# Two blocks of mLSTM, Fourier, mixer and attention layers: the order of the first loads, where rms scaling is applied, and how modulation rows are gathered

## The reference, cut to what matters

```python
sh, sc, g = jnp.split(silu(c) @ w_ada[0] + b_ada[0], 3, axis=-1)        # c: (1, 1024), w_ada[0]: (1024, 3072)
h = rmsnorm(x, norm_g[0]) * (1.0 + sc[:, None, :]) + sh[:, None, :]
shc, scc, gc = jnp.split(silu(c_ctx) @ w_ada[0] + b_ada[0], 3, axis=-1)
hc = rmsnorm(ctx, norm_g[0]) * (1.0 + scc) + shc
# rmsnorm(x, g) = x * rsqrt(mean(x*x) + 1e-6) * g, the mean over the 1024 channels
xm, o_pre, z = jnp.split(hmod @ w_in, 3, axis=-1)                        # for h and for hc; w_in: (1024, 6144)
xconv = silu(conv3x3_depthwise(xm) + conv_b)                             # then q, k, gates, a chunked mLSTM scan, ...
```

## Time and profile before

| | |
|---|---|
| median of 3 runs | 1452.86 us |
| profiled execution: own time, span | 1452.27 us, 1450.5 us |
| TensorE matmul (PE) busy | 1310.4 us, 90% |
| VectorE (DVE) busy | 825.2 us, 57% |
| ScalarE (ACT) busy | 577.5 us, 40% |
| GpSimd (POOL) busy | 241.7 us, 17% |
| mean granted TensorE clock | 0.945 |
| chain that ended last | PE 80%, DVE 8%, issue 4%, ACT 2% |
| read from memory | 193.37 MB, 134 GB/s over the span |

### The profile page before, as it was taken

One profiled execution on the slowest core, in us unless ns is written; L12 is line 12 of the kernel. 1 busy time (PEld: TensorE's weight loads), 2 busy tenths in 40 slices (PEclk: granted clock), 3 DMA queues, 4 the chain that ended last, 5 costly groups with the idle time before them and its releaser, 6 DMA issues.

```text
span 1450.5 us, 23605 instructions
## 1 busy us (share of the span) xinstructions
PE 1310.4 (90%) x9584; PEld 1194.1 (82%) x9584; DVE 825.2 (57%) x1212; ACT 577.5 (40%) x872; POOL 241.7 (17%) x169
## 2 busy tenths in 40 slices
PE   2699999999996689899998989999988779899997
PEld 1489877778983479899998989999987648899996
DVE  0567663335454757654446675554469985655544
ACT  1433443324542223445235435444354244544433
POOL 0342400034460001000200121110025500011100
PEclk8799999999996889999999999999999759999999
DMA  9356321112550003454133444455523402355551
GB/s 386 136 189 239 153 87 59 58 58 77 185 183 20 1 29 122 173 182 174 59 123 139 175 145 147 175 190 187 177 99 132 145 0 88 117 176 189 186 176 57
DMA packets 28225, 195.59 MB, mean 135 GB/s; under 512 B 3176, under 2 KB 4200, under 8 KB 4848
## 3 DMA queue, kind: packets, MB, share of 16 engines
q1 hardware_dynamic: 26208, 189.80, 35.9%
q10 hardware_dynamic: 1936, 4.62, 0.9%
HBM read 193.37 MB, written 1.05 MB: 134 GB/s over the span
## 4 chain that ended last, share of the span: by engine, by line
PE 80%; DVE 8%; issue 4%; ACT 2%; DVEq 1%; POOL 0%; ACTq 0%
PE ps L381 23%; PE ps L383 23%; PE ps L382 23%; PE ps L423 3%; PE ps L587 3%; DVE acc L1771 2%; PE ps L521 1%; PE ps L524 1%; PE ps L438 1%; DVE V L1510 1%; DVE rstd L1580 1%; PE ps L575 1%; DVE wexp L1513 1%; PE ps L449 1%; ACT w_hi L804 0%
## 5 line engine op out<-in xcount | busy, mean ns | idle before, releaser
L804 ACT ACTIVATE w_hi<-ring 128x1024 fp32r<-128x1024 f32 x312 | 327.6, 1058 | 504.9 <-PE ps L383 414.7
L1287 DVE TENSOR_TENSOR w_lo<-ring,w_hi 128x1024 fp32r<-128x1024 f32 x272 | 338.6, 1253 | 321.0 <-ACT w_hi L804 320.5
L381 PE MATMUL ps<-x_hi,w_hi 128*128 128x256 f32 x1216 | 350.0, 288 | 24.8 <-DVE x_lo L1589 20.2
L382 PE MATMUL ps<-x_lo,w_hi 128*128 128x256 f32 x1216 | 348.6, 287 | 0.0
L383 PE MATMUL ps<-x_hi,w_lo 128*128 128x256 f32 x1216 | 348.5, 287 | 0.0
L381 PEld LDWEIGHTS ps<-x_hi,w_hi 128*128 128x128 f32 x1216 | 238.3, 196 | 27.5 <-issue 24.9
L382 PEld LDWEIGHTS ps<-x_lo,w_hi 128*128 128x128 f32 x1216 | 238.5, 196 | 0.0
L383 PEld LDWEIGHTS ps<-x_hi,w_lo 128*128 128x128 f32 x1216 | 238.0, 196 | 0.0
L381 PE MATMUL ps<-g_hi,w_hi 128*128 128x256 f32 x608 | 171.8, 283 | 1.8 <-POOL g_lo L1246 1.0
L383 PE MATMUL ps<-g_hi,w_lo 128*128 128x256 f32 x608 | 171.2, 282 | 0.0
L382 PE MATMUL ps<-g_lo,w_hi 128*128 128x256 f32 x608 | 170.5, 280 | 0.0
(11 more groups left out here) (296 smaller groups left out, 2170.1 us busy)
## 6 DMA issues: line engine op xcount, KB each, us to landing
ring<-in_weights SPq DMA_DIRECT2D x156, 1024.0 KB, 4.8
o_sb<-in_weights SPq DMA_DIRECT2D x10, 1024.0 KB, 6.7
z_sb<-in_weights SPq DMA_DIRECT2D x10, 1024.0 KB, 7.9
V<-in_weights SPq DMA_DIRECT2D x3, 1024.0 KB, 19.9
dft<-in_dft ACTq DMA_DIRECT2D x1, 1026.0 KB, 5.8
X<-in_x ACTq DMA_DIRECT2D x1, 1024.0 KB, 9.8
xconv<-in_ctx ACTq DMA_DIRECT2D x1, 1024.0 KB, 35.0
xconv<-in_weights SPq DMA_DIRECT2D x1, 1024.0 KB, 28.5
```

Of the source, the lines that this page charges most:

```text
L381: mm(dst, w_h, x_h, start=start, stop=False, skip_group_check=True)
L382: mm(dst, w_h, x_l, start=False, stop=False, skip_group_check=True)
L804: do(w_hi[:, q % 2, part], ring[:, q % RING, part], ACT.Copy).then_inc(S("hi_ready"), 1)
L1287: v.tensor_tensor(w_lo[:, q % 2, part], ring[:, q % RING, part], w_hi[:, q % 2, part], ALU.subtract).then_inc(S("lo_ready"), 1)
```

## The change

- SP's queue starts with x, then the context, then the modulation blocks; the two first ring slots come behind blocks 4 and 7. ScalarE's queue has c, the vectors up to the gate weights, and the constants; the gate weights and `rows` are issued behind the h tiles.
- The context lands in `ctx_room`, which is the second half of w_lo. GpSimd therefore waits, ahead of its second slot, for the scaling by rstd and for eight h tiles.
- The rows of all early blocks are gathered in one bank (5), those of all late ones in another (6): silc is a 62-column tile with its two filled columns at 30, and block `at` uses the 32 columns from 30 - 2 at, so that its two rows come out at 2 at in each row group, and all blocks add up. There is one copy and one turn for all early blocks and one for all late ones; `fold` has 32 columns.
- The sum of squares stands behind block 2. ScalarE rounds the first ring slot ahead of the modulation's copy.
- VectorE multiplies X and context by rstd in four operations of 128 x 1024 ahead of modulation; then ScalarE makes the hi part with scale and bias in one operation, and VectorE makes the same by tensor_scalar into xconv and subtracts.

```diff
+        ctx_room = tensors(ctx_stack)("ctx_room", (P, 2, KD, CTX))[:, 1]       # shares w_lo's place
@@ SP
+            sp.dma_start(X[:, :, :], x_in).then_inc(S("x_ready"), 16)
+            sp.dma_start(ctx_room, ctx_in).then_inc(S("ctx_ready"), 16)
             for a in range(N_ADA0):
                 load_ada(a)
-                if a in (5, 7):
-                    load((a - 5) // 2)
+                if a in (4, 7):
+                    load((a - 4) // 3)
@@ TensorE
-                if a >= 2:
-                    pe.wait_ge(S("ada_moved"), a - 1)
+                late = a >= N_ADA0
+                at, count = (a - N_ADA0, N_ADA1) if late else (a, N_ADA0)
                 for j in range(2):
                     for g in range(4):
-                        last = mm(ps[32 * g:32 * g + 32, 5 + a % 2, 0:SEQ], silc[:, 4 * j + g, :],
-                                  w[:, 4 * j + g, :], start=(j == 0), stop=(j == 1), skip_group_check=True)
+                        last = mm(ps[32 * g:32 * g + 32, 5 + late, 0:SEQ],
+                                  silc[:, 4 * j + g, 30 - 2 * at:62 - 2 * at], w[:, 4 * j + g, :],
+                                  start=(at == 0 and j == 0), stop=(at == count - 1 and j == 1),
+                                  skip_group_check=True)
...
+                n = 2 * (N_ADA1 if late else N_ADA0)
                 for b in range(2):
-                    col = 2 * (2 * a + b)
-                    last = mm(ps[:, 4, col:col + 2], arow[:, a % 2, b * P:(b + 1) * P], fold[:, :],
+                    col = (4 * N_ADA0 if late else 0) + n * b
+                    last = mm(ps[:, 4, col:col + n], arow[:, b * P:(b + 1) * P], fold[:, 0:n],
                               start=True, stop=True)
...
             for a in range(N_ADA0):
                 ada_rows(a)
-                if a:
-                    ada_turn(a - 1)
-                if a == 5:
+                if a == 2:
                     pe.wait_ge(S("ones_ready"), 3)
                     column_sum(ps[:, 7, :], ones_d[:, :], lambda k: V[:, k, :], KD, S("squares_0"),
                                S("meansq_0"))
-            ada_turn(N_ADA0 - 1)
+            ada_turn(0)
...
                     ada_rows(a)
-                    if a > N_ADA0:
-                        ada_turn(a - 1)
-            ada_turn(N_ADA0 + N_ADA1 - 1)
+            ada_turn(1)
@@ ScalarE
             act.dma_start(vec[:, 0:2 * KD], vec_in[:, 0:2 * KD]).then_inc(S("c_ready"), 16)
-            act.dma_start(X[:, :, :], x_in).then_inc(S("x_ready"), 16)
+            act.dma_start(vec[:, 2 * KD:gate_at], vec_in[:, 2 * KD:gate_at]).then_inc(S("vec_ready"), 16)
             act.dma_start(cst[:, :], cst_in).then_inc(S("ident_ready"), 16)
-            act.dma_start(xconv[:, 0:KD, 0:CTX], ctx_in).then_inc(S("ctx_ready"), 16)
-            act.dma_start(vec[:, 2 * KD:VECS], vec_in[:, 2 * KD:VECS]).then_inc(S("vec_ready"), 16)
-            act.dma_start(rows[:, :], row_in).then_inc(S("rows_ready"), 16)
...
+            hi(STARTS["xm"])
+            move_rows(0)
+            act.wait_ge(S("mod0_ready"), 1)
             for k in range(KD):
-                if k in (0, 3):
-                    hi(STARTS["xm"] + k // 3)
+                if k == 4:
+                    hi(STARTS["xm"] + 1)
                 for t, col, dst in ((0, 1, hc), (1, 0, hl)):
-                    act.wait_ge(S("scaled_0"), 2 * k + t + 1)
+                    act.wait_ge(S("rooted_0"), 2 * t + k // 4 + 1)
                     do(dst[:, 0, k, :], V[:, k, t * CTX:t * CTX + SEQ], ACT.Identity,
-                       bias=modl[:, k, col:col + 1]).then_inc(S("h_rounded"), 1)
+                       bias=modl[:, k, col:col + 1], scale=scl[:, t * KD + k:t * KD + k + 1])\
+                        .then_inc(S("h_rounded"), 1)
+            act.dma_start(vec[:, gate_at:VECS], vec_in[:, gate_at:VECS]).then_inc(S("gate_w_ready"), 16)
+            act.dma_start(rows[:, :], row_in).then_inc(S("rows_ready"), 16)
@@ GpSimd
-            for q in range(STARTS["xm"], STARTS["qk"] + 2):
+            lo(STARTS["xm"])
+            pool.wait_ge(S("rooted_0"), 4)
+            pool.wait_ge(S("h_ready"), KD)
+            for q in range(STARTS["xm"] + 1, STARTS["qk"] + 2):
                 lo(q)
@@ VectorE
             chain.step(v.reciprocal(rstd[:, :], rstd[:, :]))
+            chain.join()
...
+            for t, src in enumerate((ctx_room, X)):
+                for h in range(2):
+                    k = slice(KD // 2 * h, KD // 2 * (h + 1))
+                    v.tensor_tensor(V[:, k, t * CTX:t * CTX + SEQ], src[:, k, :],
+                                    wide(rstd[:, t * CTX:t * CTX + SEQ], KD // 2), ALU.mult)\
+                        .then_inc(S("rooted_0"), 1)
...
-            dve.wait_ge(S("ada_turned"), N_ADA0)
+            dve.wait_ge(S("ada_turned"), 1)
...
+            sources = [(k, *a) for k in range(KD) for a in ((0, 1, hc), (1, 0, hl))]
+            for n in range(2 * KD + 1):
+                if n < 2 * KD:
+                    k, t, col, dst = sources[n]
+                    cols = slice(t * CTX, t * CTX + SEQ)
+                    chain.step(v.tensor_scalar(xconv[:, k, cols], V[:, k, cols],
+                                               scl[:, t * KD + k:t * KD + k + 1], modl[:, k, col:col + 1],
+                                               ALU.mult, ALU.add))
+                if n:
+                    chain.join(1 if n < 2 * KD else 0)
+                    k, t, col, dst = sources[n - 1]
+                    dve.wait_ge(S("h_rounded"), n)
+                    v.tensor_tensor(dst[:, 1, k, :], xconv[:, k, t * CTX:t * CTX + SEQ], dst[:, 0, k, :],
+                                    ALU.subtract).then_inc(S("h_ready"), 1)
```

More of the change, by code:

```diff
@@ L191, in program @@
         xconv = sa("xconv", (P, KE, TOK))
-        silc, ones_row = one_place("ones_row", (HEADS, CTX), ("silc", (P, KD, 32), F32))
-        gate_parts, arow = one_place("arow", (P, 2, SEQ), ("gate_parts", (P, 2, 2 * HC, 32), F32R))
+        arow, ones_row = one_place("ones_row", (HEADS, CTX), ("arow", (P, SEQ), F32))
+        silc, gate_parts, _ = one_place("gate_room", (P, 2, 2 * HC, 32), ("silc", (P, KD, 62), F32),
+                                     ("gate_parts", (P, 2, 2 * HC, 32), F32R))
         gcol = sa("gcol", (P, 2, 4, HEADS))
-        fold = sa("fold", (P, 2))
+        fold = sa("fold", (P, 32))
         wexp = [wexp2[:, b] for b in range(2)]
@@ L887, in silu @@
                     do(a, a, ACT.Silu).then_inc(S("xconv_ready"), 1)
-            def move_rows_of(t):
-                for a in range(2):
-                    move_rows(N_ADA0 + 2 * t + a)
             for t in range(N_XM - 2):
@@ L895, in _ @@
                 move_xm(t // 2, t % 2)
-                move_rows_of(t)
                 if t >= 2:
@@ L912, in _ @@
                 move_xm(N_XM // 2 - 1, u)
-                move_rows_of(N_XM - 2 + u)
                 if u == 0:
                     round_head(0)
+                else:
+                    move_rows(1)
                 silu(N_XM // 2 - 2, u)
@@ L924, in round_gate_weights @@
             def round_gate_weights(hd):
+                if hd == 0:
+                    act.wait_ge(S("gate_w_ready"), 16)
                 if hd >= 2:
```

72 lines of the change are left out of this document (28 added, 44 removed).

## The result

The changed kernel takes **1431.07 us** (median of four runs, 1429.36 to 1432.05) against 1452.55 (four runs, 1451.67 to 1453.43): ratio 0.9852, interval 0.9841 to 0.9864, 21.5 us less. The forecast was 1424, with a range of 1419.5 to 1430, so the time lies 1.1 us outside it. The profiled execution has a span of 1429.3 us against 1450.5, so 21.2 of the forecast 28.7 us came.

The account below looks back on a forecast made before the run. TensorE's list bounds the kernel, with a chain of waits from the late context tile before the first projection. 20.25 + 0.65 + 0.93 + 6.5 + 0.4 = 28.7 us off 1452.27 gives 1423.5, as a median 1424; range 1419.5 to 1430.

Parts of the forecast that it names:

- Loads, sum, modulation: Ahead of the first projection: context lands at 8.5 to 9, block 7 at 33.7, sum takes 8.7, modulation ready at 39.2.
- Start: TensorE's first projection matmul: at 41.05 instead of 61.30, 20.25 us gained.
- Slot 0: First xm slot, 96 matmuls: 13.55 us instead of 14.2 with the same cold start, 0.65 gained; bounds 11.8 and 15.4.
- GpSimd's next pair: GpSimd's two subtractions for the second slot: in practice behind the whole h loop, done at 54.7, covered by 4 us.
- Rival (b): Sum at 1.2 GHz (+4.9), reciprocal excluded (+2.4), or GpSimd inside h loop (up to +1.9): 1426 to 1431 us; chance 0.14.
- the bound 15.4: Upper bound in us for the first xm slot, with GpSimd taking its turns inside the h loop.
- Slots 0 to 7 and their blocks: Modulation blocks behind the xm slots: fewer turns gain 0.93, 6.5 and 0.4 us; the period falls to 13.6.
- Behind qk: Everything after qk's start: the same list, moving as a block, with no further gain or loss.

Follow-up runs that it names:

- the operands of before: Against the changed kernel with scalar_tensor_tensor and no stall: both VectorE h-loop operations read two whole tensors and a scalar per partition; 1425.86 us.
- the run without a gap: Against the changed kernel: ScalarE's second w_hi is rounded behind all sixteen h tiles instead of ahead of the ninth; 1430.94 us, ratio 0.985.

## Why the prediction was wrong, step by step

- *Loads, sum, modulation.* Right. Context landed by 8.77 (8.5 to 9), block 7 by 33.48 (33.7), the sum took 7.80 (8.7, bounds 6.9 and 13.6). The reciprocal ran its 3.35 us with a GpSimd subtraction beside it, the second subtraction cost the products 2.1, and VectorE was through at 38.08 (38.8). By the Trainium skill's rule ("SBUF — State Buffer", "Who interferes with whom") a VectorE operation with a single SBUF input doesn't contend with GpSimd outside the 2-port modes, which the page says tensor_scalar can enter. For the reciprocal the trace agrees. The prediction left out the page's exception, and it matters: tensor_scalar, with one SBUF tensor, took 2.46 us at 47.02 beside GpSimd. Start: 20.87 gained against 20.25.
- *Slot 0: the term that failed.* "With the same cold start I get 13.55: 0.65 gained", bounds 11.8 to 15.4; it took 20.25, 6.05 lost. The step under it: "GpSimd's next pair stands behind eight h tiles and in practice behind the whole loop". I took that practice from GpSimd's request of before, where VectorE's operations read two tensors and a scalar; the change puts others in their place, and these let it in. Rival (b) had the mechanism, at 0.14, but with "up to +1.9", one turn, as has the bound 15.4, and on the condition of a gap, which the run without a gap refutes. It was three turns of about 2 us each, and then the second cold start. Holding GpSimd back brought slot 0 to 13.7 us and gave 8.1 us in all, and the operands of before alone 2.5 us of slot 0 from one kernel to the other with a milder case (two turns).
- *Slots 0 to 7 and their blocks.* Right: from the end of slot 0 to qk 97.94 us against 106.34 before, 8.40 gained, 7.83 forecast.
- *Behind qk.* "The list is the same and moves as a block" was not quite so: 1.25 us lost between qk's start and the first head's first matmul (183.96 against 205.94, 21.98 gained), 0.92 of it the wait for VectorE, and 0.8 further on, of the size of the difference between runs.
- Sum: 28.7 + 0.62 (start) - 6.70 (slot 0) + 0.57 (slots) - 1.25 - 0.78 = 21.2, the difference of the spans.

The prediction priced no part alone, except that its terms for the slots, 0.93 + 6.5 + 0.4, are the gathering's. Measured, the loads are worth 20.7 us and the gathering 7.4 more (11.6 alone). The scaling under the loads is worth nothing that could be told from zero, and it is what brought in the operations that opened the row.

## What to carry to other kernels

A request of one engine that was harmlessly kept waiting is not a property of the two engines but of the very operations in the row: if a change rewrites these, price each of the other engine's waiting operations once more, as if each were let in at once, at full length. Where a helper engine's next work is not needed soon, let it ask late; one constant in a semaphore wait was worth 8 us here, 6.6 of them seen in slot 0. And try the parts of a change alone: two of the three gave 28 us, and the third, as it was built, took 7 of them back.

## What the runs showed of the hardware

- GpSimd's subtraction (2.35 us when alone) was kept out for up to 7.9 us by a row of VectorE operations that read two SBUF tensors and a scalar per partition, and let in within 0.4 to 0.7 us by rows of tensor_scalar, tensor_tensor, or scalar_tensor_tensor with a plain number or a repeated column. In two rows with own waits (71.55 in one kernel, 155.35 in another) it was let in at the last two operations of the first kind. Once in, it and VectorE alternate, one whole operation each: some 2.5 us per VectorE operation of 128 x 256.
- The Trainium skill ("SBUF — State Buffer", "Who interferes with whom") gives the shared pair to whoever starts first, for the whole instruction. The turns of 2.5 us agree. Which rows let a waiting GpSimd start at all is read from the runs above alone.
- TensorE, at full clock to 50, was granted 1.2 GHz again before 52. Ahead of that it had stood still for 1.66 us (to 49.97) and then worked again, with one gap of 0.28 us. It stayed at 1.2 GHz to 58 and was back at 2.4 GHz (0.93 as the mean of 58 to 60) behind work without a break from 54.55.
- ScalarE's rounding of 128 x 256 is 0.49 us apart with a scale and a shift per partition (the changed kernel), 0.40 with the shift alone (before).
